# TensorE's second pack inside the middle packs' loop, the later rounds behind the other side of the branch, and dummy products in hardware loops

## What is computed

```
pg_top, g_idx = lax.top_k(softmax(hf @ w_route_group + b_route_group), 1)      # one of 4 groups
pe_top, e_idx = lax.top_k(softmax(le_sel), TOP_K_INNER)                        # two of its 8 experts
weights = pg_top * pe_top
...
for e in range(N_EXPERTS):                                                     # 32
    a = jax.nn.silu(hf @ w_gate[e]) * (hf @ w_up[e])                           # 1024 -> 512
    out = out + combine[:, e:e + 1] * (a @ w_down[e]).astype(f32)              # 512 -> 1024
...
return rms_norm(x, norm_final)
```

## Time and profile before

| | us |
|---|---|
| median of 3 runs | 696.66 |
| lowest and highest | 695.86, 697.30 |
| the profiled execution: its time | 695.63 |
| the profiled execution: its span | 693.7 |

### The profile page before, as it was taken

The page is one execution under the profiler, slowest core; times in us unless marked ns, Lnnn a source line. Parts: engine busy times, 40 slices in busy tenths (PEclk is TensorE's granted clock), DMA queues, the critical chain, the costliest instruction groups (busy, mean ns, idle before and its releaser), DMA issues.

```text
span 693.7 us, 7732 instructions
## 1 busy us (share of the span) xinstructions
PE 537.6 (77%) x3339; PEld 329.7 (48%) x3339; DVE 206.7 (30%) x458; ACT 66.8 (10%) x138; POOL 43.5 (6%) x73
## 2 busy tenths in 40 slices
PE   8999999999999999898648382494567448249685
PEld 7888888888888575362232140141113114014242
DVE  4898996969523133010000010010000001000002
ACT  3010000002011022110010000010001001001002
POOL 6001111111100021000000000000000000000000
PEclk9999999999999999999879697789779779778999
DMA  8970804274179949999999999999999999999994
GB/s 333 420 320 13 351 1 135 108 262 177 47 313 428 377 187 344 436 429 428 453 421 433 419 442 435 442 423 435 427 438 446 431 423 435 427 438 442 400 430 193
DMA packets 10830, 241.81 MB, mean 349 GB/s; under 512 B 1457, under 2 KB 1585, under 8 KB 3634
## 3 DMA queue, kind: packets, MB, share of 16 engines
q1 hardware_dynamic: 10368, 239.83, 82.1%
q10 hardware_dynamic: 434, 1.58, 0.6%
HBM read 240.35 MB, written 1.05 MB: 348 GB/s over the span
## 4 chain that ended last, share of the span: by engine, by line
PE 49%; DMA 48%; DVE 1%; SPq 1%; issue 0%; ACT 0%; POOL 0%; PEldq 0%; DVEq 0%
DMA all_slots<-in_middle 40%; PE bank L1228 27%; PE bank L1514 8%; DMA all_slots<-in_last_left 5%; PE bank L1368 4%; DMA all_slots<-in_mix 3%; PE bank L1558 2%; PE bank L1217 2%; PE bank L1627 1%; PE bank L1580 1%; PE bank L1334 1%; PE bank L1470 1%; PE bank L1346 1%; PE bank L1590 1%; PE bank L1392 0%
## 5 line engine op out<-in xcount | busy, mean ns | idle before, releaser
L1228 PE MATMUL bank<-all_slots 128*128 128x256 f32 x896 | 196.1, 381 | 0.7 <-DMA all_slots<-in_mix 0.7
L1228 PEld LDWEIGHTS bank<-all_slots 128*128 128x128 f32 x896 | 169.9, 190 | 26.2 <-issue 1.3
L1506 PE MATMUL bank<-all_slots,work_region 128*32 128x512 f32 x768 | 90.8, 628 | 62.1 <-DMA all_slots<-in_middle 59.4
L1514 PE MATMUL bank<-all_slots,work_region 128*32 128x512 f32 x384 | 54.7, 733 | 52.2 <-DMA all_slots<-in_middle 52.2
L1506 PEld LDWEIGHTS bank<-all_slots,work_region 128*32 128x32 f32 x768 | 25.3, 116 | 123.3 <-DMA all_slots<-in_middle 65.0
L1138 DVE TENSOR_TENSOR work_region<-work_region,bank 128x512 f32<-128x512 f32 x8 | 8.2, 1029 | 183.5 <-PE bank L1506 150.2
L1514 PEld LDWEIGHTS bank<-all_slots,work_region 128*32 128x32 f32 x384 | 13.4, 131 | 89.5 <-DMA all_slots<-in_middle 46.9
L1143 DVE COPY work_region<-bank 128x512 f32<-128x512 f32 x7 | 4.8, 692 | 127.2 <-PE bank L1514 111.7
L1470 PE MATMUL bank<-work_region,h_region 128*128 128x128 f32 x256 | 32.9, 284 | 9.8 <-issue 9.8
L1470 PEld LDWEIGHTS bank<-work_region,h_region 128*128 128x128 f32 x256 | 31.8, 200 | 14.5 <-issue 14.5
L1368 PE MATMUL bank<-all_slots,work_region 128*128 128x512 f32 (+1 forms) x80 | 29.3, 512 | 0.0
(11 more groups left out here) (226 smaller groups left out, 423.4 us busy)
## 6 DMA issues: line engine op xcount, KB each, us to landing
all_slots<-in_mix SPq DMA_DIRECT2D x16, 2048.0 KB, 10.3
all_slots<-in_first SPq DMA_DIRECT2D x12, 2048.0 KB, 13.3
all_slots<-in_w_gate SPq DMA_DIRECT2D x2, 2048.0 KB, 9.7
all_slots<-in_middle SPq DMA_DIRECT2D x1, 4096.0 KB, 16.8
all_slots<-in_last_slices SPq DMA_DIRECT2D x1, 4096.0 KB, 39.8
all_slots<-in_last_slices SPq DMA_DIRECT2D x2, 2048.0 KB, 46.6
all_slots<-in_last_left SPq DMA_DIRECT2D x2, 2048.0 KB, 38.0
all_slots<-in_mix SPq DMA_DIRECT2D x4, 512.0 KB, 7.0
```

The source lines that it names most:

```text
L1228: ins = MM(dst, w[:, k, n * P:(n + 1) * P], rhs[:, k, :], start=k == 0, stop=k == kn - 1)
L1506: ins = MM(bank[to][quarter(e), :], xT[:, k, quarter(e)], of_expert[e][:, FF * k:FF * k + FF], start=k == 0, stop=k == KD - 1)
L1514: ins = MM(bank[6 + h][quarter(e), :], actT[:, c, quarter(e)], of_expert[e][:, D * c + 512 * h:D * c + 512 * h + 512], start=c == 0, stop= ...
```

## The change

Four edits, all in `block_kernel`:

1. `keep_clock` with n of 8 or more becomes a hardware loop of n rounds with one dummy in each; smaller n stay written out. That makes loops of six places: three of 9 rounds in `first_pack`, two of 8 in `last_gate_up`, one of 8 in `last_down`.
2. `spread_gain` runs between the first and the second pack, no longer between the second and the third. ACT's two copies of the gain move with it.
3. The load of `most` and the branch move ahead of the second pack. The branch is turned round: the side for at most 32 tokens stands first, and on it the second pack is the first round of the middle packs' loop, after waits for all four of its gate units.
4. The other side of the branch holds the second pack written out, the further rounds, the loop for packs 3 to 7 and a second copy of the last pack.

SP's program stays as it is, and so do DVE's and POOL's.

```diff
@@ (in ACT's program)
-                if pk == 1:
+                if pk == 0:
                     for h in range(2):
                         act.wait_ge(fin_psum, h + 1)
                         nc.scalar.activation(g_fin[:, 512 * h:512 * h + 512], bank[4 + h][:], ACT.Copy).then_inc(fin_ready, 1)
@@ (in PE's program)
             def keep_clock(to, n):
 
-                for _ in range(n):
+                if n < 8:
+                    for _ in range(n):
+                        MM(bank[to][:, 0:P], ident[:], ident[:], start=True, stop=True)
+                    return
+                with pe.Fori(0, n) as _:
                     MM(bank[to][:, 0:P], ident[:], ident[:], start=True, stop=True)
@@
             first_pack()
-            whole_pack(0, OVER_AT, expert_units, second_loaded)
             spread_gain()
+
+            def middle_packs(from_pack):
+                with pe.Fori(from_pack, PACKS - 1) as pk:
+                    whole_pack(0, pk + 1, expert_units, loaded_in_turn(pk))
+
             pe.wait_ge(most_ready, 1)
             most_r = pe.value_load(most[0:1, 0:1], min_val=0, max_val=T)
-            with pe.If(most_r > SLOTS):
+            with pe.If(most_r <= SLOTS):
+                for v in range(units_before(1), units_before(1) + PACK):
+                    expert_loaded(v)
+                middle_packs(1)
+                last_gate_up()
+                last_down()
+            with pe.Else():
+                whole_pack(0, OVER_AT, expert_units, second_loaded)
                 over_experts()
                 pe.sem_inc(over_done, 1)
-            with pe.Fori(OVER_AT, PACKS - 1) as pk:
-                whole_pack(0, pk + 1, expert_units, loaded_in_turn(pk))
-            last_gate_up()
-            last_down()
+                middle_packs(OVER_AT)
+                last_gate_up()
+                last_down()
```

## The result

| | before | after |
|---|---|---|
| median of 14 runs each, on the same chip, us | 695.77 | 697.95 |
| lowest and highest, us | 694.33, 697.30 | 696.03, 699.63 |
| the profiled execution: time and span, us | 695.63, 693.7 | 698.72, 696.8 |

The ratio is 1.003, with a 95% interval of 1.0018 to 1.0041: the changed kernel is slower by 1.3 to 2.9 us, which reaches past the 0.2% that the forecast took as the bound of "no change". (Ratios and intervals are estimated from all runs of both kernels and need not equal the quotient of the medians; two executions far outside the rest, 1938 us of before and 3095 us of the kernel with the early branch, are left out of them.)

The account below looks back on a forecast made before the run. The prediction took the unbroken weights' stream and the last 23.6 us as bounds; terms 0 + 0 + 0.3 + 0 gave 695.9 us against the profiled execution, and 697.0 with the runs' median 1.03 above it; range 695.6 to 701.5.

Parts of the forecast that it names:

- no change: Whole kernel: forecast 697.0 us counted as no change, within some 0.2% or 1.4 us; chance of the same 0.57.
- What bounds the kernel: Weights' stream from 277 us on: DMA engines never idle; only early transfers' slack and the last 23.6 us can count.
- The price of a loop round: Dummy loops on PE: 0.55 us a round, bounds 0.40 and 0.65, against 0.246 for a written-out dummy.
- Loops in the first pack: First pack's end moves from 303.6 to about 309.5 us; the transfer it releases is still early; price 0.
- Granted clock of 0.50 inside the first pack's down: First pack's down products: a granted clock of 0.50 there was listed as a sign of the forecast being wrong.
- Gain and branch ahead of the second pack: Second pack: gather at about 319 us, third pack's first transfer issued at 331 to 333; price 0, 0 to 2 us left.
- The decision point of 333: Third pack's first transfer: an issue after 333 us makes the end later by each us, never given back.
- the rival of a dry stream: Third pack's first transfer: issued late, weights' stream runs dry once; 698.5 to 703 us, 700 for the middle; chance 0.22.
- What goes: Ahead of the third pack's gather: the branch's 7.9 us vanish, but nothing is late because of it; value 0.
- The last pack: Last pack's tail: first down part at 671.0 us, second at 676.1 against 675.82, set by the loop; +0.3 us.
- The jump at the end: Program's end: PE's jump over the other side, 7.9 us among weights, counted as covered by 5.8 to 6.9 us; price 0.
- the jump at the end isn't covered: Program's end: rival in which PE's jump over the other side is not covered; 698.0 us, chance 0.08.

Follow-up runs that it names:

- the kernel with the early branch: The changed kernel with load of `most` and branch directly behind the first pack, sides swapped, gain's products copied into both sides; 696.55 us, ratio 1.0009 to before.
- the warm tail: The kernel before with 8 more dummies in the last pack, between the activations' transposes and the wait for their copy; 695.50 us, ratio 0.9996.
- after again: The changed kernel, unedited, timed once more beside other kernels; 696.83 us, ratio 1.0026 to before.
- the swapped kernel: The changed kernel with the branch's sides in the other order, so the jump comes ahead of the second pack's gather; 701.68 us, ratio 1.0091 to before.
- the loops alone: The kernel before with only the rows of 8 and 9 dummies made hardware loops; 696.33 us, ratio 1.0002 to before.
- the late jump: The changed kernel with PE waiting for the output to land before it leaves the branch; 699.36 us, ratio 1.0048 to before.

## Why the prediction was right, and where it was not

The time, 697.95, lies in the range and 1 us above the forecast of 697.0. That closeness flatters it: the forecast stood on the median of three runs, 696.66, and over fourteen runs before has 695.77. Against the median of its own batch the change costs 2.2 us where the sum said 0.3, and the case that had most of the chance, no change, missed by a little: it is 0.3% slower.

- **What bounds the kernel.** Right. The stream and the last stretch were the two places; every cost that a run showed was in one of them.
- **The price of a loop round.** Mis-sized: 0.55 us forecast, 0.39 measured. The loops' sequencer steps in after, all six loops:

```profile
L1220 PEldq ALU_OP  x51: 36/36/42, 290.4 to 675.9; - x51
L1220 PEldq COMPARE_BRANCH  x51: 76/208/363, 290.5 to 676.0; - x51
```

  The eight rounds behind part 6 have their register operations from 665.13 to 667.86, 0.39 us apart. A round goes like this: 0.10 from the start of the register operation to that of the branch, 0.21 for the branch, and 0.08 for the four array instructions. So two terms were too large. "0.70 / 16 = 44 ns each" is 20 ns here: it took a whole stretch behind a wait for the price of handing the instructions out. The back edge, 0.38, is 0.30: it had in it the way to the long loop's first step and a branch of 0.235. The round ended near the lower bound, 0.40, that the sum had named, and that the Trainium skill's figure ("Advanced Engine Details and Errata", Control Flow Timing, about 108 ns for a compare-and-branch) had led to, though the branch itself takes twice that.
- **Loops in the first pack.** Forecast 309.5 for the end of its down products, measured 306.0 at PE, and the gain's load is issued 2.4 us later than before (305.14 against 302.73). Most of that isn't the loops' doing: 0.8 comes from the stretch ahead of the experts and 1.3 from the first down part, which takes 3.26 us in place of 1.92, at the low clock, behind waits of 1.2 and 0.7 us that stand in before too:

```profile
290.60:294.00 3.40, 3.40 (x19) 1.06 (x12) 0.00 (x0) 0.00 (x0) 0.00 (x0) 0.50 1.03 443
```

  (Columns as in the earlier trace rows.) "Granted clock of 0.50 inside the first pack's down" was one of the signs of being wrong, and it came; but it comes with written-out dummies as well (the warm tail in the kernel before: 3.4 us at 0.50 from 290.3, the gain's load issued at 304.90), and after again has it not (load issued at 302.38, as in before). So it differs between executions; what decides it, no run shows. The sequencer is ahead of PE in these loops, so that 9 rounds take PE 2.2 us, as written out (2.5 the first time).
- **Gain and branch ahead of the second pack.** The chain of waits of after, its PE timeline behind it, and SP's issue:

```profile
305.14 7.27 DMA work_region<-in_norm_final
```

```profile
312.45 1.98 PE L1675 MATMUL bank<-work_region,ones 1*128 1x512 f32 x4 [2.52 <-DMA work_region<-in_norm_final]
316.57 2.07 PE L1474 MATMUL bank<-work_region,h_region 128*128 128x128 f32 x8 [2.15 <-issue]
318.44 0.64 PE L1482 MATMUL bank<-ident,work_region 128*128 128x128 f32 x2
318.86 4.03 PE L1474 MATMUL bank<-work_region,h_region 128*128 128x128 f32 x24
323.73 7.07 PE L1510 MATMUL bank<-all_slots,work_region 128*32 128x512 f32 x64 [0.84 <-DVE work_region L1135]
```

```profile
330.95 7.71 SPq L499 DMA_DIRECT2D all_slots<-in_middle  x2
```

  The gain lands 7.3 us after its issue (forecast 6; 6.3 to 8.5 in the runs), the gather starts at 316.57 (forecast 319), and the third pack's first transfer is issued at 330.95 (forecast 331 to 333). Errors of opposite sign lie in that agreement, the rounds too dear, the load too cheap and the low clock in the first pack left out, so it is in part luck. (The landing of the output, 3.0 us, from which the prediction takes its "about 2 us", is the one in the section on the result; the earlier trace rows doesn't have it.) The decision point of 333 was too late by some 1 us: the runs put it between 331.3 and 332.4. In the kernels of after's shape, this issue came at 326.4 (high clock through the first pack, 3.4 us of low clock behind it) to 332.4 (13.7 us of low clock from 309.9 on). So the price of 0 holds for most of these profiles and is some tenths of a us for the late one, and the rival of a dry stream, 0.22, was the right one to fear: the swapped kernel shows it at its full price.
- **What goes.** Right. The branch at 316 is not taken and takes 80 ns, the 7.9 us are gone, and nothing got faster by it.
- **The last pack.** Forecast +0.3 for the second down part, measured in the chain of after:

```profile
665.11 3.21 PE bank L1221 x16
...
672.77 1.92 PE bank L1631 x16
674.69 1.98 PE bank L1221 x16
676.67 1.90 PE bank L1631 x16
```

  It starts at 676.67 against 675.82, 0.85 later. The first part runs at the high clock, 1.92 us, as forecast, but starts at 672.77 and not at 671.0, because parts 5 and 6 ahead of it had begun later and ran slower (5.34 us in place of 3.64, with 3.4 us at a granted clock of 0.50 from 655.9 on, behind a wait of 2.6 us for weights); the loop then has its rounds handed out in time (1.98 us, as written out), where the sum had let it set the pace. The loop behind part 6 does set PE's pace (3.21 us, where the written-out row takes 2.02). So the sum's +0.3 has the right sign and not the right way: The 0.85 of this execution is made up otherwise: PE comes to the turning of the activations 4.1 us later (1.3 for the start of part 5, 1.7 for the low clock in parts 5 and 6, 1.1 for the loop behind part 6), of which a shorter wait ahead of the first down part gives back 1.6 and its high clock 1.7. The low clock in parts 5 and 6 comes with written-out dummies as well (5.34 us in the warm tail). With the loops alone in the kernel before, the second down part started at 675.23, some 0.5 us earlier than in before.
- **The jump at the end.** This is the step that failed: "without the weights' traffic, which has stopped, I count it as covered". The cover was reckoned for PE's sequencer alone, and by that it holds (3.3 us used of 5.8). The jump's fetches were not weighed as transfers, and the second of them stands in one DMA engine's way while the output goes through it: +2 us in all four profiles with a jump there, and in none without. The rival "the jump at the end isn't covered", 698.0 at a chance of 0.08, has the right place and size but another mechanism; only the late jump turned it into the kernel's actual end. The Trainium skill's rule ("Runtime: NRT & Kernel Launch", Instruction fetch mechanics) that a taken branch out of the fetched window waits for a fetch was borne out in each such row, 3.3 to 7.9 us. What the runs add is that the fetch also takes time from data transfers.

## What to carry to other kernels

In these runs a far jump has two prices: the sequencer's stall, and the code blocks that go through the DMA engines beside data. Price both where it stands, and keep such a jump out of the stretch in which the output is written, or put it where the engine waits anyway. When a term is called covered, ask what else the covered work uses.

## What the runs showed of the hardware

- A far jump of PE takes 3.3, 3.6, 3.6, 3.8 and 3.8 us at the program's end, where hardly anything else moves, and 5.8 to 7.9 us beside the stream of weights (425 to 440 GB/s; eight profiles). How much code is jumped over does not show in it: beside the weights some 120 products took 6.2 to 7.9 us, the other side of the branch, up to some 500, took 5.8 to 6.6. A branch that isn't taken takes 80 ns, a back edge 208 ns.
- Such a jump brings two code blocks of 16 KB, the second after the jump is over. Beside the 1 MB output it delays the last packets by 2 us: one engine of sixteen finishes alone, at 24 GB/s. No row names the engine, but the packet records do settle that it is the one with the code block (15.4 packets under way in place of 16.4, and the late packets start when the block ends).
- A load of 4 KB takes 6.3 to 8.5 us beside the weights.
- In the experts' stretch the granted clock fell to 0.50, for 3.4 us or more, at places that differ between executions and don't go with the edits: at 290.6 us in after, at 290.3 in the warm tail with its first pack unedited, and not there in after again. What decides the place, no run shows.
